# GpSimd's weight-splitting subtraction in pieces of 256 columns instead of one instruction of 1024 (two stacked blocks, one core)

## The reference

```python
ada = c_act @ w_ada + b_ada
proj = jnp.einsum("bsd,dp->bsp", u, w_in)
a = causal_depthwise_conv(a, conv_a_w) + conv_a_b          # 31 taps
q = jnp.einsum("bsr,rk->bsk", rms_norm(q_lat, q_norm_g), w_uq)
o = causal_block_attention(qf, kf, v).reshape(b, s, MLA_WIDTH)
m = g_a * y_a + g_b * y_b + g_c * y_c
out = jnp.einsum("bsd,de->bse", m, w_o)
...
xm, o_pre, z = jnp.split(hmod @ w_in, 3, axis=-1)
xconv = lax.conv_general_dilated(xg, conv_w, (1, 1), 'SAME', ...)   # 3x3 taps
q = jnp.einsum('bnhd,hde->bhne', xh, w_q)
k = jnp.einsum('bnhd,hde->bhne', xh, w_k) * (DH ** -0.5)
```

## Time and profile before

| | before |
|---|---|
| median of 3 runs | 2640.37 us (2639.97 to 2640.83) |
| span of the profiled execution | 2636.6 us |
| around the span, if that execution took the median | 3.8 us |
| TensorE (PE) busy | 2328.1 us, 88% |
| VectorE (DVE) busy | 1575.8 us, 60% |
| ScalarE (ACT) busy | 855.3 us, 32% |
| GpSimd (POOL) busy | 796.8 us, 30%, of which line 371: 306 instructions of 2508 ns on average |
| DMA | 259.8 MB, mean 99 GB/s |

### The profile page before, as it was taken

The page is one execution under the profiler, slowest core; times in us unless marked ns, Lnnn a source line. Parts: engine busy times, 40 slices in busy tenths (PEclk is TensorE's granted clock), DMA queues, the critical chain, the costliest instruction groups (busy, mean ns, idle before and its releaser), DMA issues.

```text
span 2636.6 us, 29830 instructions
## 1 busy us (share of the span) xinstructions
PE 2328.1 (88%) x10776; PEld 1882.7 (71%) x10776; DVE 1575.8 (60%) x2328; ACT 855.3 (32%) x1394; POOL 796.8 (30%) x326
## 2 busy tenths in 40 slices
PE   3898889899889898899976889888599999899997
PEld 1677667788568676688755778777477777688875
DVE  4689987542568997844248574752658657523311
ACT  1242234222433223422244333323333333432312
POOL 1233223344333322334422232321132332233332
PEclk8999999999989989999988999999699999999999
DMA  7343322553233222243411222221242341222222
GB/s 274 96 126 103 103 92 84 176 158 94 86 121 100 81 89 71 76 138 110 135 49 64 80 89 86 72 94 60 89 136 80 112 128 56 76 72 72 72 72 64
DMA packets 93202, 259.79 MB, mean 99 GB/s; under 512 B 10128, under 2 KB 11536, under 8 KB 92944
## 3 DMA queue, kind: packets, MB, share of 16 engines
q1 hardware_dynamic: 67552, 202.89, 24.6%
q10 hardware_dynamic: 25520, 55.13, 5.9%
HBM read 237.01 MB, written 20.97 MB: 98 GB/s over the span
## 4 chain that ended last, share of the span: by engine, by line
PE 44%; issue 25%; DVE 20%; POOL 6%; ACT 4%; ACTq 1%; DMA 0%; POOLq 0%; DVEq 0%; SPq 0%
PE bank L1817 14%; PE bank L1818 13%; PE bank L1819 13%; POOL t L371 6%; DVE t L1516 5%; DVE t L1313 3%; DVE t L1048 1%; DVE t L1678 1%; DVE t L1044 1%; DVE t L1105 1%; PE bank L1898 1%; PE bank L1885 1%; DVE t L1052 1%; PE bank L2167 1%; DVE t L1513 0%
## 5 line engine op out<-in xcount | busy, mean ns | idle before, releaser
L1817 PE MATMUL bank<-t,t 128*128 128x512 f32 (+2 forms) x3072 | 1200.7, 391 | 131.2 <-DVE t L1052 25.0
L371 POOL TENSOR_TENSOR t<-t,t 128x1024 fp32r<-128x1024 f32 x306 | 766.5, 2508 | 1629.3 <-ACT t L405 1629.1
L1818 PE MATMUL bank<-t,t 128*128 128x512 f32 (+2 forms) x3072 | 1170.3, 381 | 0.0
L1819 PE MATMUL bank<-t,t 128*128 128x512 f32 (+2 forms) x3072 | 1167.3, 380 | 0.0
L1817 PEld LDWEIGHTS bank<-t,t 128*128 128x128 f32 x3072 | 595.1, 194 | 268.1 <-DVE t L1052 29.5
L1818 PEld LDWEIGHTS bank<-t,t 128*128 128x128 f32 x3072 | 595.2, 194 | 109.5 <-issue 5.3
L1819 PEld LDWEIGHTS bank<-t,t 128*128 128x128 f32 x3072 | 592.6, 193 | 110.5
L405 ACT ACTIVATE t<-t 128x1024 fp32r<-128x1024 f32 x306 | 321.3, 1053 | 240.9 <-PE bank L1819 206.4
L1313 DVE SCALAR_TENSOR_TENSOR t<-t,t,t 128x512 f32<-128x512 f32 x240 | 247.6, 1032 | 6.7
L1105 DVE SCALAR_TENSOR_TENSOR t<-t,t,t 128x512 f32<-128x512 f32 x168 | 159.1, 960 | 100.3 <-DMA t<-w_ada 83.6
L1048 DVE SCALAR_TENSOR_TENSOR t<-t,bank 128x512 f32<-128x512 f32 x112 | 76.7, 685 | 193.8 <-PE bank L1819 97.2
(11 more groups left out here) (224 smaller groups left out, 1771.6 us busy)
## 6 DMA issues: line engine op xcount, KB each, us to landing
t<-blocks SPq DMA_DIRECT2D x306, 512.0 KB, 3.7
t<-w_ada SPq DMA_DIRECT2D x144, 256.0 KB, 2.8
t<-w_ada ACTq DMA_DIRECT2D x16, 512.0 KB, 12.3
xm_park<-t ACTq DMA_DIRECT2D x16, 384.0 KB, 2.3
s_park<-t ACTq DMA_DIRECT2D x16, 384.0 KB, 2.3
t<-xm_park ACTq DMA_DIRECT2D x16, 384.0 KB, 4.6
t<-s_park ACTq DMA_DIRECT2D x16, 384.0 KB, 5.2
t<-w_ada SPq DMA_DIRECT2D x8, 512.0 KB, 14.8
```

The lines of the kernel that those rows point to most:

```text
L371: pool.tensor_tensor(w_lo[slot][:], w_raw[slot][:], w_hi[slot][:].bitcast(F32), ALU.subtract).then_inc(weights_lo, 1)
L1817: pe.matmul(out, wh, xh, start=start, stop=False)
L1818: pe.matmul(out, wh, xl, start=False, stop=False)
L1819: return pe.matmul(out, wl, xh, start=False, stop=stop)
```

## The change

Each of the 306 subtractions of 1024 columns becomes four of 256, and each of the 16 of 768 columns becomes three of 256. The waits stay in front of the first piece; the semaphore is raised by the last.

```diff
 BLK = 1024
+POOL_PIECE = 256
 RING = 3
...
             def low_part(b, slot):
                 pool.wait_ge(weights_hi, b + 1)
-                pool.tensor_tensor(w_lo[slot][:], w_raw[slot][:], w_hi[slot][:].bitcast(F32),
-                                   ALU.subtract).then_inc(weights_lo, 1)
+                for i in range(0, BLK, POOL_PIECE):
+                    part = slice(i, i + POOL_PIECE)
+                    low = pool.tensor_tensor(w_lo[slot][:, part], w_raw[slot][:, part], w_hi[slot][:, part].bitcast(F32), ALU.subtract)
+                low.then_inc(weights_lo, 1)
...
                             pool.wait_ge(act_done, A("xcH", h, c))
-                            pool.tensor_tensor(xcL[:, c, :], c_acc[c % 2][:], xcH[:, c, :].bitcast(F32), ALU.subtract)\
-                                .then_inc(xc_low, 1)
+                            for i in range(0, SEQ, POOL_PIECE):
+                                part = slice(i, i + POOL_PIECE)
+                                low = pool.tensor_tensor(xcL[:, c, part], c_acc[c % 2][:, part], xcH[:, c, part].bitcast(F32), ALU.subtract)
+                            low.then_inc(xc_low, 1)
```

## The result

| | before | after |
|---|---|---|
| median | 2640.17 us (2637.63 to 2640.83, 4 runs) | 2559.77 us (2556.29 to 2562.03, 4 runs) |
| ratio | | 0.9693, 95% interval 0.9679 to 0.9706 |
| span of the profiled execution | 2636.6 us | 2560.0 us |
| TensorE, VectorE, GpSimd busy | 2328.1, 1575.8, 796.8 us | 2313.6, 1451.9, 1067.7 us |
| mean granted clock of TensorE | 0.946 | 0.952 |

Code lines are now 3 to 5 numbers later: L1318 is the tap that was L1313, L1110 was L1105, L1057 was L1052, L1649 was L1644, L1521 was L1516, L374 was L371 and L391 was L386.

What follows compares the result with a forecast made beforehand. VectorE, held up by GpSimd's subtractions, was taken to set the pace in the attention phases. Terms of 24, 7.6, 7, 5, 8 and -1.3 us summed to 50.3, so 2640.4 - 50 = 2590 us, range 2560 to 2637.

Steps and rivals of the forecast that it cites:

- Alternation and its price: Where both engines are dense: one tap, one piece in turn, round 1.16 us, VectorE losing 0.37 us per piece; chance 0.64.
- Rival 2: GpSimd's next piece goes before the waiting tap, VectorE stands for all four, 2.8 us; 2671 us; slower, mostly this, 0.09.
- Rival 1: Handing over eats the gain: a turn costs 0.49 instead of 0.37 us, dense stretches gain nothing; 2620 to 2635 us; chance 0.13.
- the row at 213 us: Attention phase, kernel before: a tap recorded 0.05 us ahead of a subtraction still waited 2.2 us; priced 1.5 us per block.
- Attention phases, 12 a phase: Two attention phases: VectorE loses less per subtraction, gaining 13 us a phase, taken as 12; 24 in all (10 to 40).
- About three of four meet one, 1.15: Attention phases: about three of a block's four pieces meet a VectorE instruction, costing 1.15 us instead of 1.70 per subtraction.
- End of the gated branch, 3.8 a layer: Two held-up low parts of line 1052, TensorE waiting 7.0 us for the second: 3.8 us a layer, 7.6 in all.
- Readout, 8 us: Readout of the heads: TensorE's four waits for line 1656, 12.9 us, shrink; gain 8 us (4 to 10).
- mLSTM projections, 5 us: Dense taps: a pair of xcL and block costs 2.6 instead of 3.4 us; gain 5 us (-5 to 10).
- Single hits 7: Short chains, line 1240 at 134 us and line 1052 at 2523 us: each gains 1.3 to 1.5; 7 us (3 to 10).
- GpSimd on the path -1.3: Start and two later places where TensorE needs three low parts: pieces take longer; -1.3 us (-4 to 0).
- rival 4: Much more: each hit costs only one piece's remainder, other terms at upper ends; up to 80 us, 2560; chance 0.07.

## Why the prediction was right and wrong

- **Alternation and its price: right.** Round of 1.14 us (1.16 predicted), 0.34 us lost per piece (0.37), a piece alone 0.74 at the median (0.68, the choice of 2.8 for four was nearer). Rival 2, GpSimd keeping the interface, would show taps of 2.8 us; none of line 1318 is over 1.24, none of line 1521 over 1.32. Rival 1 would leave the mean of the taps unchanged; it fell from 1088 to 847 ns. One reading was too narrow. By the row at 213 us I set aside the rule that whoever is first goes first. In that row the recorded starts are only 0.04 us apart (213.36 and 213.41, rounded). Over the whole trace of before, 54 taps and sums of `w_ada` start 0.06 to 0.6 us ahead of a subtraction with nothing in their way; all 54 took their usual 0.75 us, and it was the subtraction that grew longer. The changed kernel has 44 of 44. Held up were those recorded at most 0.04 us ahead, or behind. VectorE, then GpSimd, in the kernel before:

```profile
166.03 0.75 DVE L1105 SCALAR_TENSOR_TENSOR t<-t,t,t 128x512 f32<-128x512 f32 x1
```

```profile
166.10 2.95 POOL L371 TENSOR_TENSOR t<-t,t 128x1024 fp32r<-128x1024 f32 x1 [0.69 <-ACT t L405]
```

- **Attention phases, 12 a phase: the step that failed most.** "About three of four meet one, 1.15" was nearly right: 2.7 instructions are held up for each block, for 1.0 us a block in the first phase and 1.06 in the second. What was too small was the gain worked out around it. The price before, 1.70 us a subtraction, counted three lines (39 us); over all lines it was 1.82 and 1.85 (41.9 and 42.6), most of the rest on line 1380. With 22 and 24 us instead of 26 lost after, VectorE gains 19.8 and 18.7 us a phase, not 13. I also took 12 for 13 because TensorE's room was "little at the phase's beginning"; 166 against 186 us shows that all of VectorE's gain became length. 42 instead of 24: 18 of the missing 30 us. The changed kernel's timeline at 246 us shows a block of which three pieces hold something up, GpSimd's four pieces and then VectorE's instructions beside them:

```profile
246.60 4.27 POOL L374 TENSOR_TENSOR t<-t,t 128x256 fp32r<-128x256 f32 x4 [2.78 <-ACT t L410]
```

```profile
244.00 4.26 DVE L1318 SCALAR_TENSOR_TENSOR t<-t,t,t 128x512 f32<-128x512 f32 x5
248.18 0.96 DVE L1106 TENSOR_SCALAR t<-t,t 128x512 f32<-128x512 f32 x1
249.24 1.03 DVE L1110 SCALAR_TENSOR_TENSOR t<-t,t,t 128x512 f32<-128x512 f32 x1
```

  The fourth tap had started 0.25 us before the first piece and kept its 0.75 us; that piece took 1.10. The fifth tap took 1.11, line 1106 0.96 (0.48 by itself) and line 1110 1.03 (0.75).
- **End of the gated branch, 3.8 a layer: too small.** The waits shrank by 5.0 and 5.2 us in the two layers, and what TensorE gained by the granted clock after them (0.77 to 0.99 in 15 us), 1.0 and 2.8 us, was in no term at all. 15 instead of 7.6. The same omission concerns every term in which a long wait of TensorE ends; how much of the other terms it makes was not measured apart.
- **Readout, 8 us: too small.** The wait named went from 12.9 us in four places to 7.0, 5.9 us against the 8 of the term. A second one, which the prediction did not read, went with it. The kernel before and the changed one, waits in this stage:

```profile
PE bank L1817 <- DVE t L1052: 5.8, 4, 1.5
```

```profile
PE bank L2336 <- DVE t L1661: 7.0, 1, 7.0
```

  The three small ones behind line 1656 are gone, as are the four behind line 1052; a listing of the one largest wait was too short a reading of a stage of 400 us.
- **mLSTM projections, 5 us: right in size** (6.9, interval 4.5 to 10.6 from the ratio; 5 by the changed kernel's own trace). The two parts of the term were not measured apart.
- **Single hits 7, and GpSimd on the path -1.3: not borne out.** The kernel with pieces in both layers gained 59.2 us, those for attention and branch alone 57.0 together: 2.2 us are left for the two hits of the layers and the start, less than the runs' uncertainty. Line 1240 itself did what the term said, from 2435 ns at most to 1144 (now line 1245), but TensorE's waits for it went from 8.2 to 9.0 us. By ScalarE's instructions the changed kernel is 1.8 us ahead at 140 us and level again at 170, and by the starts of the first tap, 1.6 us came out before 173 us. TensorE's waits for line 374 before 100 us are 6.5 us where they were 2.8 for line 371: the pieces eat part of it there, as expected, and somewhat more.
- **The range.** Its low end was rival 4's "up to 80 us, 2560", to which I gave 0.07 beyond 75 us. That is the edge at which the time came out, and not by other physics: the three large terms all came out above their own upper ends (42 against 40 for attention, 15 against 10, 13 to 17 against 10), pushed there by losses of VectorE that were not counted, by the clock and by a wait that was not read. Each of the three had left out something that added to the gain, so the sum of their upper ends was no far corner.

## What to carry to other kernels

Where VectorE and GpSimd share a reading path, look for durations far above the median of the same form, and cut the instruction of the engine with slack, not the one that is waited for; the right length depends on the stage: small (128 columns here) where VectorE is dense and the consumer has time, long where the next engine waits for the product, never so small that the producer runs without a pause. When a wait of TensorE goes away, count the time of the same matmuls in the stretch after it too, and try the expected gain stage by stage: here the gains of the stages, each measured by itself, added up to the whole.

## What the runs showed of the hardware

- **GpSimd's subtraction has a fixed part of about 0.18 us.** Alone it takes at least 2333 ns for 1024 columns (the lines below), 1255 for 512, 713 for 256 and 446 for 128: 2.1 ns per column, and 0.17 to 0.18 us over. For 64 columns this gives 0.31, and the shortest of the 768 such pieces takes 310 ns, half of them at most 326; the 0.48 each of the long row at 199.64 us hold turns of VectorE.

```profile
L371 POOL TENSOR_TENSOR t<-t,t x306: 2333/2402/2947, 55.3 to 2605.8; 128x1024 fp32r<-128x1024 f32 x153
...
L374 POOL TENSOR_TENSOR t<-t,t x612: 1255/1295/3346, 55.8 to 2562.3; 128x512 fp32r<-128x512 f32 x153
...
L374 POOL TENSOR_TENSOR t<-t,t x2448: 446/462/2237, 55.4 to 2515.6; 128x128 fp32r<-128x128 f32 x189
```

- **GpSimd waits for a long VectorE instruction just as much.** The one piece of 256 that took 2809 ns lies beside a two-input instruction of VectorE (line 1049) on 2064 columns. In the changed kernel at 2182 us, GpSimd, then VectorE:

```profile
2182.09 2.81 POOL L374 TENSOR_TENSOR t<-t,t 128x256 fp32r<-128x256 f32 x1
```

```profile
2181.44 2.85 DVE L1049 TENSOR_TENSOR t<-t,t 128x2064 fp32r<-128x2064 f32 x1
```

  The piece ends 0.60 us after it. Splitting VectorE's own long instructions was not tried.
- **Who goes first.** A tap or sum of `w_ada` recorded 0.06 to 0.6 us ahead of GpSimd's subtraction passes at its usual 0.75 us, 98 times of 98 in the two kernels, and one recorded at most 0.04 us ahead is held up, 14 of 14. Where both have work waiting they take turns, one instruction each.
- **A fill on GpSimd holds up some of VectorE's work.** Beside fills of 0.95 us, 240 taps with two large inputs kept at most 790 ns; a tensor_scalar of line 1312 took 1064 ns instead of 546.
- **What a read-free GpSimd is worth.** Replacing 306 reads of two blocks by fills took 6.7% off the kernel before. How much of this is the meetings and how much GpSimd's shorter part was not told apart.
